# Paged sample attention scored two batches at a time, with other key buffers and another interleaving

## What is computed

```python
def sparse_attend(q, k_sel, v_sel, valid):
    s = jnp.einsum('bthd,btkhd->bthk', q, k_sel) * (HEAD_DIM ** -0.5)
    s = jnp.where(valid[:, :, None, :], s, -jnp.inf)
    p = jax.nn.softmax(s, axis=-1)
    return jnp.einsum('bthk,btkhd->bthd', p, v_sel)
# sample batch b: 8 queries, 8 heads of 64; keys = 16 pages of 128 tokens from cache_k / cache_v
# (page_table[b]), then the 8 new tokens; valid = the top 256 keys of the indexer
```

## Time and profile before

| what | value |
|---|---|
| median of 3 runs | 1527.69 us (1525.25 to 1529.77) |
| the profiled execution | 1532.19 us, span 1530.5 us |
| PE busy | 1469.0 us, 96% of the span |
| DVE, ACT, POOL busy | 911.6, 500.1, 533.4 us |
| attention stage, last projection matmul to first recurrence matmul | 749.3 to 1046.2 us |
| share of PE on the chain that ended last | 80% |
| DMA busy share in the attention stage | about 0.8, at 260 to 290 GB/s |

### The profile page before, as it was taken

One profiled execution on the slowest core, in us unless ns is written; L12 is line 12 of the kernel. 1 busy time (PEld: TensorE's weight loads), 2 busy tenths in 40 slices (PEclk: granted clock), 3 DMA queues, 4 the chain that ended last, 5 costly groups with the idle time before them and its releaser, 6 DMA issues.

```text
span 1530.5 us, 30636 instructions
## 1 busy us (share of the span) xinstructions
PE 1469.0 (96%) x11472; PEld 1353.3 (88%) x11472; DVE 911.6 (60%) x1676; ACT 500.1 (33%) x955; POOL 533.4 (35%) x564
## 2 busy tenths in 40 slices
PE   9999988999999999999899999988899999999998
PEld 8999978999999999999767666667888999999998
DVE  6357522699999999500266666658974564028222
ACT  6256422122133100012256656662025313333110
POOL 6522352245533314515022222221643354323110
PEclk9999999999999999999999999999979999999999
DMA  6021232122232322201387788864025542223011
GB/s 217 19 78 58 83 93 79 45 100 72 99 136 108 114 94 97 72 19 59 108 284 257 251 284 281 276 219 147 1 91 162 180 151 92 84 83 104 34 38 35
DMA packets 116757, 183.78 MB, mean 120 GB/s; under 512 B 23105, under 2 KB 76162, under 8 KB 116610
## 3 DMA queue, kind: packets, MB, share of 16 engines
q1 hardware_dynamic: 104834, 146.69, 28.8%
q0 software_dynamic: 11776, 35.14, 6.9%
HBM read 147.95 MB, written 33.83 MB: 119 GB/s over the span
## 4 chain that ended last, share of the span: by engine, by line
PE 80%; DVE 7%; SPq 4%; issue 4%; ACT 3%; DMA 1%; POOL 1%; ACTq 0%; DVEq 0%; POOLq 0%
PE PS L1100 29%; PE PS L1522 13%; PE PS L1107 7%; PE PS L1177 4%; PE PS L1141 3%; PE PS L1320 2%; PE PS L1356 2%; PE PS L1312 2%; PE PS L1332 2%; SPq L705 2%; PE PS L1282 2%; SPq L706 2%; PE PS L1303 2%; PE PS L1382 2%; ACT buf L1788 1%
## 5 line engine op out<-in xcount | busy, mean ns | idle before, releaser
L1999 DVE TENSOR_SCALAR_CACHE_REDUCE buf<-buf,buf 128x384 f32<-128x384 f32 (+6 forms) x224 | 243.4, 1153 | 1.1
L1100 PE MATMUL PS<-hn_lo,w_hi 128*128 128x384 f32 x720 | 234.8, 326 | 0.0
L1100 PE MATMUL PS<-hn_hi,w_lo 128*128 128x384 f32 x720 | 234.7, 326 | 0.0
L1100 PE MATMUL PS<-hn_hi,w_hi 128*128 128x384 f32 x720 | 234.6, 326 | 0.0
L924 POOL CAST w_hi<-buf 128x2048 fp32r<-128x2048 f32 (+2 forms) x43 | 77.8, 1808 | 424.9 <-DMA buf<-in_w_in_dram 138.4
L928 POOL TENSOR_TENSOR w_lo<-buf,w_hi 128x512 fp32r<-128x512 f32 (+1 forms) x153 | 220.0, 1438 | 12.1
L1522 PE MATMUL PS<-w_hi,mix_hi 128*128 128x256 f32 (+1 forms) x576 | 164.5, 286 | 1.0 <-DVE mix_lo L2182 1.0
L1522 PE MATMUL PS<-w_lo,mix_hi 128*128 128x256 f32 (+1 forms) x576 | 162.9, 283 | 0.0
L1522 PE MATMUL PS<-w_hi,mix_lo 128*128 128x256 f32 (+1 forms) x576 | 162.8, 283 | 0.0
L691 POOL DMA_DIRECT2D buf<-in_cache_v_dram x128 | 73.0, 570 | 243.3 <-PE PS L1356 134.5
L1788 ACT ACTIVATE buf<-PS 128x512 f32<-128x512 f32 (+4 forms) x200 | 101.5, 507 | 109.3 <-PE PS L1312 67.2
(11 more groups left out here) (290 smaller groups left out, 3283.3 us busy)
## 6 DMA issues: line engine op xcount, KB each, us to landing
buf<-in_cache_k_dram SPq DMA_DIRECT2D x128, 256.0 KB, 4.6
buf<-in_cache_v_dram POOLq DMA_DIRECT2D x128, 256.0 KB, 4.8
buf<-in_w_in_dram SPq DMA_DIRECT2D x26, 1024.0 KB, 5.9
gates_scratch<-buf SPq DMA_DIRECT2D x40, 544.0 KB, 3.0
buf<-gates_scratch SPq DMA_DIRECT2D x40, 544.0 KB, 5.1
buf<-in_x_prompt_dram SPq DMA_DIRECT2D x16, 512.0 KB, 4.1
out_dram<-buf SPq DMA_DIRECT2D x34, 128.0 KB, 1.7
out_dram<-buf SPq DMA_DIRECT2D x2, 2048.0 KB, 7.7
```

Of the source, the lines that this page charges most:

```text
L1100: last = mm(ps[0:min(w, P), 512 * j:512 * j + tn], wt[:, k, P * half:min(w, P * half + P)], xt_[:, k, t0:t0 + tn], start=m == 0, stop=m == ...
L1999: run(V.tensor_scalar(marks[j][0:r], v, t, None, op, ALU.add, accum_out=CN[0:r, j:j + 1]), ch, wait=j == NJ - 1)
```

## The change

It does these things:

- **Pairs.** Entries S, X, P, M and O now stand for a pair of batches (`NPR` = 4). `Qz` puts the even batch in rows 0 to 15 of each group of 32 and the odd one in rows 16 to 31; S runs eight key matmuls, accumulated for u = 0 and 1, and one mask matmul. X and P run once per pair. V stays one entry for each batch and chunk, into columns 0:128 or 128:256 of bank 7. M scales twice, O has two matmuls. `head_of`, `row_of` and `sel_b` get constants to match.
- **Buffers.** `KTb` has three buffers (`NKT`), `outm` two. Six of the eight key page buffers (`NEARLY`) lie outside the projections' operands: four of them take the place of value page buffers. `NVP` falls from 14 to 10. SP loads six key pages before the projections end, after waiting for `topk_bias`.
- **Order.** The pages of a pair alternate by chunks of four. Entries have weights: K 2, S 2, P 1, V 8 (0 for the short last chunk), all others 0. `some` hands out weight in place of entries (572 in all, 17.9 a round), and an entry of weight 0 follows at once. The loads of the recurrence's rows come at S entries x = 0 and 2 of the last two pairs.

```diff
+        halves = [(c, u) for c in range(NPG // 4) for u in range(2)]
+        page_at = [(2 * p + u, 4 * c + g) for p in range(NPR) for c, u in halves for g in range(4)]
...
+        for p in range(NPR + 1):
+            for j in range(len(halves) + 1):
...
+                if j % 2 == 0 and p >= 1:
+                    smp_plan += [("P", p - 1, j // 2)]
+                if j % 2 == 0 and j and p < NPR:
+                    smp_plan += [("S", p, j // 2 - 1)] + ([("S", p, j // 2)] if j == len(halves) else [])
+                if j and p >= 1:
+                    c, u = halves[j - 1]
+                    smp_plan += [("V", 2 * (p - 1) + u, c)]
...
+        weight = {e: {"K": 2, "S": 2, "P": 1, "V": 8 * (e[2] < n_pch - 1)}.get(e[0], 0) for e in smp_plan}
...
-        kpage = [xk(AW) for _ in range(2)] + near[:NKP - 2]
-        vpage = near[NKP - 2:] + [xv(AW) for _ in range(4)]
+        NKP, NEARLY = 8, 6
+        kpage = [xk(AW) for _ in range(2)] + [xv(AW) for _ in range(4)] + near[:NKP - NEARLY]
+        vpage = near[NKP - NEARLY:]
...
-            for x in range(2):
-                page_load(sp, kpage[x], ck, 0, x, sem(f"kpage_load{x}"))
+            sp.wait_ge(sem("topk_bias"), NJ)
+            for n in range(NEARLY):
+                page_load(sp, kpage[n], ck, *page_at[n], sem(f"kpage_load{n}"))
...
-                    for k in range(HP):
-                        keys = KTb[x % 2][:, k, :] if x < 4 else KT[:, k, SEQ:NT]
-                        mm(o[32 * k:32 * k + 32, 0:w], Qz[:, k, b, :, :].rearrange("p h q -> p (h q)"), keys,
-                           start=True, stop=False, skip_group_check=True)
+                    for u in range(2):
+                        for k in range(HP):
+                            keys = KTb[page_no[2 * b + u, 4 * x] // 4 % NKT][:, k, :] if x < 4 else KT[:, k, SEQ:NT]
+                            mm(o[32 * k:32 * k + 32, 0:w], Qz[:, k, 2 * b + u, :, :].rearrange("p h q -> p (h q)"), keys,
+                               start=u == 0, stop=False, skip_group_check=True)
                     mm(o[:, 0:w], sel_b[0:NS, b, :, :, :].rearrange("p k h q -> p (k h q)"),
                        mb_s[0:NS, c:c + w], start=False, stop=True, skip_group_check=True)\
...
+                    for u in range(2):
+                        run(V.scalar_tensor_tensor(out=outm[u], in0=bank(7)[:, P * u:P * u + P], scalar=sri,
+                                                   in1=head_of[u], op0=ALU.mult, op1=ALU.mult), sem("smp_outm"))
```

More of the change, by code:

```diff
@@ L91, in hybrid_layer @@
         levelm = take(1024).bitcast(u8).rearrange("p (l h t) -> p l h t", l=8, h=HH)
-        head_of = take(P)
+        head_of = [take(P) for _ in range(2)]
         row_of = take(HP * TS)
-        sel_b = take(BS * P // 2).bitcast(bf16).rearrange("p (b k h q) -> p b k h q", b=BS, k=HP, h=4)
+        sel_b = take(NPR * P // 2).bitcast(bf16).rearrange("p (b k h q) -> p b k h q", b=NPR, k=HP, h=4)
         q_eq = take(64)
@@ L525, in hybrid_layer @@
         n_pch = (NPB + 3) // 4
+        halves = [(c, u) for c in range(NPG // 4) for u in range(2)]
+        page_at = [(2 * p + u, 4 * c + g) for p in range(NPR) for c, u in halves for g in range(4)]
+        page_no = {bg: n for n, bg in enumerate(page_at)}
         smp_plan = []
[L527 to L540, removed]
+        for p in range(NPR + 1):
+            for j in range(len(halves) + 1):
+                if j < len(halves) and p < NPR:
+                    c, u = halves[j]
+                    for g in range(4 * c, 4 * c + 4):
+                        smp_plan += [("K", 2 * p + u, g)] + ([("X", p - 1, 1)] if p >= 1 and (j, g) == (0, 1) else [])
+                if (p, j) == (NPR, 0):
+                    smp_plan += [("X", p - 1, 1)]
+                if j == 0 and p >= 2:
+                    smp_plan += [("O", p - 2, 0)]
+                if j % 2 == 0 and p >= 1:
[5 more added lines that the diff above has]
+                    smp_plan += [("V", 2 * (p - 1) + u, c)]
+                    if j == len(halves):
+                        smp_plan += [("V", 2 * (p - 1) + u_, n_pch - 1) for u_ in range(2)]
+            smp_plan += ([("M", p - 1, 0)] if p >= 1 else []) + ([("X", p, 0)] if p < NPR else [])
+        smp_plan += [("O", NPR - 1, 0)]
         def turns(n):
@@ L546, in hybrid_layer @@
         plan = []
-        n_smp = sum(e[0] not in "MX" for e in smp_plan)
+        weight = {e: {"K": 2, "S": 2, "P": 1, "V": 8 * (e[2] < n_pch - 1)}.get(e[0], 0) for e in smp_plan}
+        n_smp = sum(weight.values())
         given = [0, 0]
@@ L552, in some @@
             given[0] += share
-            while given[1] < len(smp_plan) and (sum(e[0] not in "MX" for e in smp_plan[:given[1] + 1])
-                                                <= given[0] * n_smp / (8 * NM) or smp_plan[given[1]][0] in "MX"):
+            while given[1] < len(smp_plan) and (sum(weight[e] for e in smp_plan[:given[1] + 1])
+                                                <= given[0] * n_smp / (8 * NM) or not weight[smp_plan[given[1]]]):
                 plan.append(smp_plan[given[1]])
```

83 lines of the change are left out of this document (45 added, 38 removed).

## The result

The changed kernel takes 1543.43 us (median of four runs, 1540.24 to 1544.96) against 1528.18 of the kernel before, measured beside it: ratio 1.0093, 95% interval 1.0062 to 1.0124. It is 15 us slower, where 1525.1 was forecast and 1514 to 1536 given as the range. The profiled span is 1542.8 us (before 1530.5), the mean granted clock 0.976 (before 0.989). The loss lies in the attention stage: its end, the first matmul of the recurrence (L1403, before L1382), comes at 1058.24 us instead of 1046.16, and what follows takes 484.6 us instead of 484.3. One execution each of the kernel before (3421 us) and of the kernel with two early key pages (1616 us) lies far outside all others and counts in no ratio.

A forecast was written before the change was run, and what follows sets the result against it. PE was taken to bind the attention stage nearly without a break. Terms -13.1 - 3.5 + 5.5 + 8.5 = -2.6 us gave 1529.6 us profiled, median 1525.1 us; own range 1519 to 1531, with outer rivals 1514 to 1536.

The forecast's parts named there:

- Work (-13.1): PE in the attention stage: fewer mask matmuls (5.1 us) and halved P transposes (8.0 us) count in full, -13.1 us.
- Start (-3.5): Stage start: six early key pages bring the ninth page at 760 to 761 us, -3.5 us, ends -7 and +3.
- Boundaries (+5 for waits): Four pair boundaries: PE waits for ACT's copies behind X, 15.5 us against 10.7 before, +5 us.
- The clock (+0.5): Pair boundaries: lower granted clock behind PE's waits, charged +0.5 us.
- The end (+8.5): Last pair's V: ten buffers leave 22 pages to POOL at its pace, PE waits +8.5 us, ends +4 and +13.
- the walk: Step-by-step working; at the end, 22 pages at POOL's pace make V end no sooner than 29.5 us after it began.
- Value pages in time: Rival at the stage's end: value pages keep up, end costs about 1 us, median about 1517 us; chance 0.27.
- First pages: Rival at the start: SP's pace holds PE through 32 pages, start +3 us, median about 1531 us; chance 0.15.
- The slower rival: PE waits of some 2 us at boundaries and last V halve the granted clock, +11 us, 1536 us; chance 0.15.

The follow-up runs named there:

- the kernel with two early key pages: Changed kernel with SP loading the last pair's odd value pages and X after both E, but two early key pages instead of six: 1526.91 us against 1524.38.
- The odd batches alone: Kernel before, with odd batches' mask matmuls and 48 transposes of P left out, nothing else changed, output not the reference's: 1518.46 us, ratio 0.9923.
- both repairs: Changed kernel with SP loading the odd value pages of the last pair and X held back until both E of its round: 1524.38 us, ratio 0.9952.
- equal weights: Changed kernel with every sample entry except M and X counting 1, POOL alone loading value pages: 1527.58 us, ratio 0.9993 to the kernel before.
- filling the waits: Changed kernel with 89 useless 128x128 identity matmuls in twelve places where PE waits: 1534.80 us, ratio 1.0024 to the kernel before.
- holding X back: Changed kernel with X held at pair boundaries until both exponentials E of the prompt round stand ahead of it on ACT: 1529.19 us, ratio 0.9986.
- half the pages on SP: Changed kernel with SP loading the odd and POOL the even value pages of the last pair: 1535.04 us, ratio 1.004 to the kernel before.
- the 28 useless matmuls: Changed kernel with SP loading odd last-pair value pages, X after both E, and 28 useless identity matmuls in the last 45 us: 1517.33 us, ratio 0.9922.
- the last pages come from two engines as well: Changed kernel with equal entry weights and SP loading the last pair's odd value pages, X after both E: 1522.03 us.

## Why the prediction was wrong

**Work (-13.1).** Right. The counts are 64 + 4 transposes of P and 16 + 4 mask matmuls; the full transposes of P are busy for 10.5 us instead of 19.8 and the masks for 6.2 instead of 12.4. The odd batches alone gave 10.3 of 10.9 us by the time of the runs (7.4 by the start of the recurrence).

**Start (-3.5).** Right in mechanism, the ninth page came at 761.5 us. Its size was measured only with both repairs, 2.5 us by the medians and 7.6 by the profiles.

**Boundaries (+5 for waits).** The waits were right. Those for ACT and for DVE's L2096 are 5.9 + 4.3 + 2.2 + 0.9 + 1.9 = 15.2 us against 15.5 in the sum. Missing was Q's wait for the bank of the short S, 3.3 us in three pieces of up to 1.2. With equal weights Q waits too, 3.9 us, but for the copy of a key page (L680): the bank's holder changes and the wait stays. Whether another order on DVE would remove it was not tested.

**The clock (+0.5): the step that failed.** The working took the boundaries' waits of 2.1 us and then charged almost nothing for what they do to the clock, giving the rival 0.15; at the end it charged nothing at all. It read the earlier trace rows as a question of the length of one wait, with 0.71 us on one side, 3.09 on the other and its own in between. But the earlier trace rows and the third row had the clock low behind shorter waits, at the last boundary of the kernel before: V took 1.93 us behind this wait of 1.14 and one of 0.88.

```profile
1027.84 1.09 PE L1343 MATMUL PS<-buf,buf 128*128 128x128 f32 x8 [1.14 <-ACT buf L1786]
```

The runs show that 2.25 and 1.81 us, three microseconds apart, bring the clock to its lower level, and so do 2.19 and 1.82 at the first boundary and 2.04 and 1.81 at the third.

How much it cost: filling the waits gave 8.6 us net, and holding X back gave 8 us beyond its 6.2 us of waits. What is left when the other terms are taken from the +12.1 us of the stage is another measure: -12.4 of work (13.1 x 10.3 / 10.9), -2.5 at the start, +15.2 - 10.7 = +4.5 of boundary waits, +3.3 for Q, +7.9 for value pages make +0.8, and 11.3 remain. That remainder is worked out and not measured by itself; with the sizes of work and start that the profiles give instead it lies between 8 and 16.

A third measure is an estimate from the rows of PE: adding up, for the rows that took over 8% longer than the shortest of the same shape and count in any of these runs, what they took beyond it gives 30.4 us in the changed kernel and 16.6 before, 13.8 more. Of these, 7.9 lie behind 1000 us, where V rows of 1.08 us take 1.94 and 2.09. So the term of +0.5 should have been about 8 to 16 us, half of it at the end. The rival's mechanism was this; that its +11 us fits so well is in part luck, since it put most of it at the boundaries.

By the Trainium skill (TensorE: Matmul & The Clock Gate, A second HAM failure mode: psum-queue depth-cycling) PE that idles briefly between groups cycling through PSUM banks can swing in clock. The three inner boundaries here agree, at waits of 1.8 to 2.3 us; the same boundaries of the kernel with equal weights alone, at 1.2 us and less, do not show it, and its last one, at 1.26, 0.92 and 1.32 us within 5 us, does (the V row behind them takes 1.94 us, like forms otherwise 1.08).

**The end (+8.5).** The mechanism and the size of the waits were right: 7.9 us. That half the pages on SP gave back 8.4 looks like a second agreement, but it is half waits and half clock. The stretch took 35.2 us instead of 29.5 (1.6 + 25.9 + 3.4 is 29.3, a slip of 0.2). The last V itself adds 2.1 us, which the walk left out. The rest is mostly a pause in POOL's list, which the walk let run without a break: 3.2 us of idle time, where 0.6 is usual. The same pause stands before the same page in the kernels with X held back and with equal weights (3.20 us each), and with useless matmuls (3.19 us, put down to no other engine). In that last kernel the clock is 1.00 from 1000 to 1040 us and the stretch still takes 33.9 us. So neither the clock nor the order of the entries makes the pause, and its cause stays open.

**The rivals.** Value pages in time: refuted by six waits for them. First pages: refuted, key pages cost 1.6 us of waiting in all. The slower rival had the cause and 1536 us; the 7 us beyond are of the order of Q's 3.3 and the longer end together, which is not a measurement.

**What the prediction did not ask.** It costed each edit with the order as it stood. The weights, a line of numbers, decide that order, and undoing them alone removes 15.9 us. The pairs with equal weights are as fast as the kernel before (0.9993), and a gain, some 7 of the about 10 us of work, shows once the last pages come from two engines as well.

## What to carry to other kernels

When a change adds waits of about 2 us on TensorE, or several of about 1 us close together, price the clock with them: look at the granted clock behind every such wait, and at the same group of matmuls at either level. If a wait can't be removed, a few useless matmuls in it can pay, but only where the clock falls behind it. And when numbers that only steer an interleaving are changed together with the work, try the work with the old numbers too: the place of one long instruction on an engine that works in order can outweigh all that was saved.

## What the runs showed of the hardware

Two waits of 2.25 and 1.81 us, 3 us apart, were enough to bring the granted clock down, and so were two such waits at every inner boundary of the changed kernel. Shorter ones could go either way. At the second boundary 1.25 and 0.87 us left it alone with six early key pages and 1.25 and 0.86 brought it down with two; at the third 1.13 and 0.86 left it alone with both repairs (eight transposes in 1.07 us) and brought it down in the same order of work with the 28 useless matmuls, which come only later (1.94 us). In the kernel before with ten value buffers it fell behind 1.51, 0.87 and 0.53 us in 5 us. So no length of wait found here decides by itself.

A page load issued by POOL landed 3.4 us later on the chain, and POOL's pace was 1.15 us a page with its reading of the page number. By the Trainium skill (DMA: Bandwidth & Descriptors, Anatomy of one DMA) it would be an estimated 2.6 us; the measurement decides.

The same instructions after the stage took 484.3 us in the kernel before and 479.6 us with equal weights (1525.2 - 1045.6). Both are rows of a stretch in the recurrence, the kernel before first:

```profile
1100.00:1200.00 100.00, 89.22 (x712) 81.46 (x711) 61.87 (x124) 39.14 (x46) 43.27 (x27) 0.90 0.38 118
```

```profile
1100.00:1200.00 100.00, 88.96 (x740) 81.95 (x739) 65.41 (x129) 44.33 (x50) 43.39 (x27) 0.95 0.42 133
```

The clock there differs from one execution to another, which is worth some 5 us, as much as the smaller effects of this study. The start of the recurrence in the profile leaves this part out, though it stems from a single execution.
